# Delta steps beside the attention squares, softmax transposes a unit later, two weight splits inside each convolution

## The reference, cut to what matters

```
xn   = rms_norm(h, attn_norm);  proj = xn @ w_in
gq, gk, gv, gz, gb, ga, mq, mk, mv = split(proj)
qkv  = silu(causal_short_conv([gq, gk, gv], conv_w))      # 4 taps
A    = strict_lower((k*beta) @ k.T * decay)               # per head and chunk
Tm   = inverse(I + A);  u = Tm @ (v*beta);  w = Tm @ (k*beta*exp(gc))
o    = gated delta rule over the chunks, then rms_norm(o) * silu(z)
attn = softmax(rms_norm(mq) @ rms_norm(mk).T * scale + causal) @ mv
h    = h + [o, attn] @ w_o
h    = h + (silu(hn @ w_gate) * (hn @ w_up)) @ w_down
h    = h + sigmoid(rms_norm(h) @ w_ple_gate) * (p @ w_ple_proj)
```

## Time and profile before

| what | value |
|---|---|
| median of 3 runs | 1355.14 us (1354.77 to 1355.86) |
| the profiled execution | 1352.64 us, of it the span from first to last instruction 1350.9 us |
| PE busy | 1329.8 us, 98% |
| PE weight loads busy | 1124.1 us, 83% |
| DVE busy | 797.7 us, 59% |
| ACT busy | 608.8 us, 45% |
| granted TensorE clock, mean | 0.999 |

### The profile page before, as it was taken

The page is one execution under the profiler, slowest core; times in us unless marked ns, Lnnn a source line. Parts: engine busy times, 40 slices in busy tenths (PEclk is TensorE's granted clock), DMA queues, the critical chain, the costliest instruction groups (busy, mean ns, idle before and its releaser), DMA issues.

```text
span 1350.9 us, 19215 instructions
## 1 busy us (share of the span) xinstructions
PE 1329.8 (98%) x7295; PEld 1124.1 (83%) x7295; DVE 797.7 (59%) x996; ACT 608.8 (45%) x756; POOL 60.7 (4%) x71
## 2 busy tenths in 40 slices
PE   7999999999999999999999999999999999999998
PEld 5999987887888888888888888888888888888886
DVE  6657887589667555555555554454555555555554
ACT  6456533452445545444444443434444444454442
POOL 4102000031110000000000000000000000000000
PEclk9999999999999999999999999999999999999999
DMA  7645454544444756666666656666666666555563
GB/s 240 185 148 172 144 179 134 141 140 139 128 125 141 236 184 187 192 191 180 195 192 187 185 192 193 191 198 191 195 188 189 190 187 187 181 193 188 186 198 129
DMA packets 126366, 240.52 MB, mean 178 GB/s; under 512 B 9743, under 2 KB 10050, under 8 KB 126298
## 3 DMA queue, kind: packets, MB, share of 16 engines
q1 hardware_dynamic: 125108, 237.46, 58.1%
q10 hardware_dynamic: 1190, 2.12, 0.5%
HBM read 237.45 MB, written 2.10 MB: 177 GB/s over the span
## 4 chain that ended last, share of the span: by engine, by line
PE 92%; DVE 5%; ACT 1%; issue 1%; DVEq 0%; ACTq 0%
PE pair L511 26%; PE pair L513 25%; PE pair L512 25%; PE pair L714 3%; PE pair L715 3%; PE pair L716 3%; PE bg L615 2%; DVE w_lo L1117 1%; PE bg L680 1%; PE bg L767 1%; PE bg L556 1%; ACT w_hi L835 0%; DVE mn L1351 0%; PE bg L595 0%; DVE mn L1272 0%
## 5 line engine op out<-in xcount | busy, mean ns | idle before, releaser
L1117 DVE TENSOR_TENSOR w_lo<-raw,w_hi 128x1024 fp32r<-128x1024 f32 x444 | 541.6, 1225 | 420.8 <-ACT w_hi L835 417.9
L835 ACT ACTIVATE w_hi<-raw 128x1024 fp32r<-128x1024 f32 x444 | 468.0, 1060 | 495.7 <-PE pair L513 457.5
L511 PE MATMUL pair<-w_hi,xT_hi 128*128 128x512 f32 x1088 | 431.7, 397 | 0.0
L513 PE MATMUL pair<-w_hi,xT_lo 128*128 128x512 f32 x1088 | 424.1, 390 | 0.0
L512 PE MATMUL pair<-w_lo,xT_hi 128*128 128x512 f32 x1088 | 423.7, 389 | 0.0
L513 PEld LDWEIGHTS pair<-w_hi,xT_lo 128*128 128x128 f32 x1088 | 204.2, 188 | 43.3
L511 PEld LDWEIGHTS pair<-w_hi,xT_hi 128*128 128x128 f32 x1088 | 204.4, 188 | 41.5
L512 PEld LDWEIGHTS pair<-w_lo,xT_hi 128*128 128x128 f32 x1088 | 204.5, 188 | 40.1
L511 PE MATMUL pair<-w_hi,actT_hi 128*128 128x512 f32 x352 | 137.7, 391 | 0.0
L513 PE MATMUL pair<-w_hi,actT_lo 128*128 128x512 f32 x352 | 137.1, 389 | 0.0
L512 PE MATMUL pair<-w_lo,actT_hi 128*128 128x512 f32 x352 | 137.0, 389 | 0.0
(11 more groups left out here) (223 smaller groups left out, 953.6 us busy)
## 6 DMA issues: line engine op xcount, KB each, us to landing
raw<-in_w_in_dram SPq DMA_DIRECT2D x112, 512.0 KB, 3.8
raw<-in_w_gate_dram SPq DMA_DIRECT2D x88, 512.0 KB, 4.4
raw<-in_w_up_dram SPq DMA_DIRECT2D x88, 512.0 KB, 3.8
raw<-in_w_down_dram SPq DMA_DIRECT2D x88, 512.0 KB, 4.7
raw<-in_w_o_dram SPq DMA_DIRECT2D x32, 512.0 KB, 4.9
raw<-in_w_ple_gate_dram SPq DMA_DIRECT2D x32, 512.0 KB, 4.6
raw<-in_w_ple_proj_dram SPq DMA_DIRECT2D x4, 512.0 KB, 7.4
h<-in_x_dram SPq DMA_DIRECT2D x4, 512.0 KB, 8.5
```

What stands on the lines that cost most here:

```text
L511: mm(banks[t][:], hi[:, ts], wh, start=first, stop=False)
L513: m = mm(banks[t][:], lo[:, ts], wh, start=False, stop=last)
L835: f(w_hi[j % RING][:], raw[j % RING][:], ACT.Copy).then_inc(hi_ready, 1)
L1117: v.tensor_tensor(w_lo[j % RING][:], raw[j % RING][:], w_hi[j % RING][:].bitcast(F32), ALU.subtract).then_inc(lo_ready, 1)
```

## The change

There are four edits.

1. `chunk_steps` has one more "rest" behind `gramA`, so `Y1` stands one slot of its block later.
2. The slots leave out the eight units in which an `m_sq` stands, and end one unit earlier. Before there were 62 pairs for 68 slots, now 64 pairs for 59 slots; so five slots hold two pairs each, where before no slot held more than one.
3. `pT` stands three units behind its `sc` instead of two. That is the unit of the next `sc`, and one before its own `pv`.
4. In the first five convolutions the splits of two units stand within the convolution (on DVE behind the first tap and behind the third, on ACT both ahead of the sigmoids), in the last one only the first of them. The pass j = 1 of the block behind loses its split in all five, since it was made already.

```diff
--- before.py
+++ after.py
@@ -79,7 +79,7 @@
 
 def chunk_steps(b):
 
-    steps = ["q_tok", "k_tok", "gcrow", "v_tok", "rest", "gramQ", "gramA"]
+    steps = ["q_tok", "k_tok", "gcrow", "v_tok", "rest", "gramQ", "gramA", "rest"]
     for l in range(1, LEVELS - 1):
         steps += [f"Y{l}", f"Z{l}"]
     steps += [f"TT{LEVELS - 2}", f"Y{LEVELS - 1}", "ZT"]
@@ -104,7 +104,9 @@
     for g in range(KT // 2):
         at[U_QKV - 1 + g // 4][g // 2 % 2].append(("x", g))
     at[U_QKV + 3][1].append(("taps", 0))
-    slots = [U_QKV + n * UPB + j for n in range(3, 6) for j in range(4, UPB)] + list(range(U_Z + 4, U_WO - 4))
+    m_units = [U_MIX + (1 + j) * UPB + 2 + t for j in range(4) for t in range(NT)]
+    slots = [U_QKV + n * UPB + j for n in range(3, 6) for j in range(4, UPB)]
+    slots += [u for u in range(U_Z + 4, U_WO - 5) if u not in m_units]
     for n, steps in enumerate(pairs):
         at[slots[n * len(slots) // len(pairs)]][1] += steps
 
@@ -118,7 +120,7 @@
     for i, u in enumerate((U_WO - 9, U_WO - 6, U_WO - 3, U_WO)):
         for k in range(2):
             at[u][k].append(("sc", 2 * i + k))
-            at[u + 2][k].append(("pT", 2 * i + k))
+            at[u + 3][k].append(("pT", 2 * i + k))
             at[u + 4][k].append(("pv", 2 * i + k))
 
     for n in range(4):
@@ -980,6 +982,8 @@
                     f(mn[m // 2][:, cs], pair[n % 2][m // 2][:, cs], ACT.Copy,
                       scale=convw[:, t0 * CONV + CONV - 1:t0 * CONV + CONV]).then_inc(tap3, 1)
                 split(u, u)
+                if n < 5:
+                    split(u + 1, u + 1)
                 for q in range(2):
                     act.wait_ge(taps, n * 12 + (10 + 2 * q))
                     f(sq[q][:], mn[q][:], ACT.Sigmoid).then_inc(conv_sig, 1)
@@ -995,7 +999,7 @@
             for n in range(6):
                 for j in range(UPB):
                     u = U_QKV + n * UPB + j
-                    if j or not n:
+                    if j > 1 or not n:
                         split(u + LEAD, u + LEAD)
                     for k in range(2):
                         for s in AT[u][k]:
@@ -1337,7 +1341,7 @@
                 kind, half = QKV_BLOCKS[n]
                 done = 0
                 for tap in (2, 1, 0):
-                    if tap == 0:
+                    if tap == 1:
                         split(u, u)
                     sh = CONV - 1 - tap
                     for m in range(4):
```

## The result

The changed kernel takes 1350.45 us in the median of 6 runs (1350.24 to 1350.84); the kernel before, in 6 runs beside it, 1355.27 (1353.65 to 1355.86). The ratio is 0.9965, with a 95% interval of 0.9955 to 0.9976: 0.35% faster, 4.8 us. The two profiled executions, 1352.64 and 1350.37 us, differ by only 2.3. So the question is where the other 2.4 us are.

What follows compares the result with a forecast made beforehand. The prediction took PE, busy 98% of the span, as the bound, with only its waits to win. Its terms, 2.35 + 0.89 + 0.43 - 0.85 - 0.4 = 2.4 us, gave 1355.14 - 2.4 = 1352.7 us, range 1350.9 to 1354.7.

Steps and rivals of the forecast that it cites:

- The free slot behind gramA: Behind units 84 and 88: PE's waits of 2.20 and 0.35 go, less 0.2 before Z1; gain 2.35 us.
- the wait that I set before `Z1`: Block 2, behind the slot of unit 81: PE waits 0.2 us for DVE, bounds 0 and 0.9.
- Unit 40: Fourth convolution: the split now stands ahead of the multiplications, so the wait before unit 40 goes; gain 0.89 us.
- Unit 51: Doubled slot with Y2, Y3, Z2, Z3: 0.98 waiting plus 0.1 at unit 56, less 0.23 saved; loss 0.85 us.
- Unit 97: Doubled slot: `u` waits 0.6 for ACT's copy of ZT, 0.2 saved; loss 0.4 us, bounds 0.2 and 1.
- the 1.3 to 1.5 I gave `Y6`: Unit 97's burst: with Y6 adding 0.4 to 0.6, PE comes to `u` at 1.3 to 1.5 us.
- Softmax: Units 109 and 110: 1.7 us of waits removed come down to a gain of 0.43, bounds 0 and 1.7.
- the wait before `ogT` of block 3: Softmax: PE comes some 0.4 us sooner and waits that long for bank 2, until `og_lo` of block 2 ends.
- The step that failed: Whole kernel: the 2.5 us between profiled execution and median was carried over, so 1355.14 - 2.4 = 1352.7 us.
- The rival "slower": Units 81 to 85: DVE's queue doesn't drain, Z1 and five slots wait 1 us each; +3 to 1358 us, chance 0.05.
- The rival "the clock": At the new waits: PE's clock falls to 1.2 GHz, one fall costing 1.6 us; 1354.3 us, chance 0.04.
- "More comes through": Units 76 to 109: DVE catches up, softmax gives 1.7, Z1 and `u` don't wait; gain 4.5, 1350.6 us, chance 0.30.

Runs made afterwards that it cites:

- experiment 1: The kernel before, unedited, profiled and timed a second time: median 1355.03 us, the profiled execution 1354.62.
- experiment 2: The kernel before with only the free slot behind gramA and the new list of slots: 1352.25 us, ratio 0.9981.
- experiment 4: The kernel before with only pT a unit later: 1354.41 us, ratio 0.9994.
- experiment 5: The kernel before with 15 throwaway matmuls of 256 columns in the pause before Y1 of block 2: 1353.59 us, ratio 0.9994.
- experiment 9: The changed kernel with PE paused in ten units, each until POOL has done four small fills: 1388.15 us, ratio 1.0249.
- experiment 3: The kernel before with only the two splits in each of the first five convolutions: 1353.72 us, ratio 0.9989.
- experiment 6: The changed kernel with PE paused once, in the middle of unit 85, for four small fills on POOL: 1354.16 us.
- experiment 10: The changed kernel with PE paused in ten units, each until POOL has done two small fills: 1368.62 us, ratio 1.0103.

## Why the forecast was half of the gain

**The free slot behind gramA** (2.35): right in its mechanism. By the starts 2.37 + 0.38 went, and the wait that I set before `Z1` did not come, so 2.75.

**Unit 40** (0.89): right, 0.89. That it would have been 1.41 with the new slots alone, I did not see; it changes nothing for the sum of the whole, since a wait of 1.41 exists in neither kernel of the comparison.

**Unit 51** (-0.85): 0.75 + 0.39 + 0.1 less 0.2 for the saved burst, -1.0. **Unit 97** (-0.4): 0.95 less 0.2, -0.75; ACT's second copy started 1.52 us behind the burst and ended at 1.9, as I had it, but `u` started at 2.04 and PE was there sooner than the 1.3 to 1.5 I gave `Y6`. **Softmax** (0.43): 0.74 + 1.28 - 1.32 = 0.7; the wait before `ogT` of block 3 did not come.

The sum of these is 2.75 + 0.89 - 1.0 - 0.75 + 0.7 = 2.6 against 2.4. But between the ends of the first and the last unit the two traces differ by 1331.99 - 1328.57 = 3.4 us (experiment 1). So 0.8 are not in my list at all. PE goes over from a product to steps 137 times in the old kernel and 129 times in the changed one: three fewer by the slots, and five fewer since `pT` stands with `sc` (experiments 2 and 4 have 134 and 132). My sum counts two of these eight, at 0.2 each, and put the others at nothing. That they make up the 0.8 is not shown.

**The step that failed** is the last of the sum: "The profiled execution took 1352.64, so 1350.2 in its terms; the median of the runs is 2.5 higher for the same kernel, and I take the difference from it." That takes the 2.5 us for something that all kernels have. They were mostly the old kernel's own: by their times 7 of 10 of its executions lose the clock for a while behind the pause (experiments 1, 5 and 9), the profiled one did not, and the changed kernel, which lacks the pause, shows no such fall in its trace and has a spread of 0.6 us. In the traces the fall took 1.4 us. The second, smaller miss is the sum itself, 2.4 for 3.4. Together, 3.4 + 1.4 = 4.8: that is the difference between the second profile of the kernel before and the changed one, 1333.41 - 1328.57, and that of the medians. Either term put right alone would have given a time inside the range: 1355.14 - 3.4 = 1351.7, or 1355.14 - 2.4 - 1.4 = 1351.3.

The forecast in the profile's terms, 1350.2, was 0.25 off the measured median. That is luck: the sum was 1.0 too small, and the changed kernel's profiled execution started 1.1 later than the old one's (13.42 against 12.28). The hint at the failed step was in the numbers: a profiled execution below all three timed runs by 2.1 us, whose own spread was 1.1.

**The rival "slower"** has a slip: five units more of 1 us and the 2.35 gone are +5 on its own terms, 1360 us, not +3 and 1358. Nothing hangs on it, since `Z1` did not wait.

**The rival "the clock"** had the mechanism, with the wrong sign: it asked whether the new waits could lower the clock, and took from one execution that the old pause does not ("Before, PE stood 2.2 us and the granted clock stayed at 1.00"). The Trainium skill (TensorE: Matmul & The Clock Gate, Part 1) says that the low clock is the default and activity lifts it, and that the point of change is not tied to the kernel's start and differs from run to run. I set the first against a single draw; by the second, one trace that shows no fall is hardly evidence against it. Experiment 9 agrees with both: 2 of 10 such pauses kept the clock, and the three runs of experiment 9 differ by 4.8 us.

**"More comes through"** (1350.6) met the time and not the reason: the softmax did not give its 1.7, and `u` waited.

What stays open: the two groups of the kernel before are 2.2 us apart in the means, of which a fall accounts for 1.4 to 1.7; and the mean of the lower group is only 1353.05 - 1350.51 = 2.5 above that of the changed kernel, where the traces have 3.4. Both would fit if the executions without a fall start sooner, as the profiled one did; but the start is known of profiled executions only, and no run separates it.

## What to carry to other kernels

Compare the profiled execution with the timed runs before anything else. If it lies outside them, or the runs fall in groups, the gap can be a term of this kernel with a cause of its own, as here, and not a constant to be carried over; profile it again before the sum is made. And compare two traces from the end of the first unit on, since the start differs by itself. Price a stop of PE at its length only where it is short: here 1.4 us cost 1.5, while 2.2 to 2.6 cost 1.4 to 1.7 more in most executions, and if such a stop can't be removed, throwaway matmuls in it can save that part. Steps that "rest" are the latency of something: before a slot is shared, ask whose.

## What the runs showed of the hardware

- The granted clock fell behind 8 of 10 pauses of 2.55 us or more in one execution, and behind none of nine of 1.39 us in another. Of the single pauses of 2.2 to 2.6 us in five profiles of other kernels here (before twice, experiments 3, 4 and 6), two were followed by a fall.
- A fall costs always the same by the granted clock: 1.7 us in each of the ten whose windows are summed here (experiments 1, 9 and 10), whether matmuls of 512 columns or small ones run in it. In time it was 1.4 us in experiment 1. The low clock shows when PE is at work again, not in the pause: the windows of the pause itself read 1.00.
- The start of the same kernel differs: PE started the last matmul of the first unit at 12.28 us in one profile of the kernel before and at 12.84 in the other, and before that point matmuls of 512 columns stand 0.43 apart up to 11.31 in the one and to 11.97 in the other.
- With 15 matmuls whose result is overwritten in the same 2.2 us, the clock stayed up in the profiled execution and none of 11 runs reached the upper group; they cost 0.12 us at the place.
